# Moving evictions and rotations, and changing two matmul shapes, in the latent attention of a two-block layer on one core

## The chip, the cores and the metric

One Trainium2 chip, of which the program uses one core. The time is that of one execution on the device in microseconds; the figure of a kernel is the median of its runs. The profile is one further execution. TensorE (PE; PEld in the views is its weight loads) multiplies, VectorE (DVE) and ScalarE (ACT) work on elements, GpSimd (POOL) and SyncE (SP) issue transfers.

## What is computed

A sequence of 256 tokens with 2048 channels goes through one block (modulation, gated spatial unit, long convolution, feed-forward) and then a second one of two layers: a pooling mixer and a latent attention. The change touches only the latter, here cut to what matters:

```python
def mla_mixer(xn, cos, sin, w_in, q_norm, w_uq, kv_norm, w_ukv, w_out):
    z = xn @ w_in                       # q_lat 512, kv_lat 512, k_pe 64, g 2048
    q = (rms_norm(q_lat, q_norm) @ w_uq).reshape(B, S, 16, 192)
    kv = (rms_norm(kv_lat, kv_norm) @ w_ukv).reshape(B, S, 16, 256)
    q_nope, q_pe = q[..., :128], q[..., 128:]
    k_nope, v = kv[..., :128], kv[..., 128:]
    q_pe = rope(q_pe, cos, sin)         # 64 channels, for each head
    k_pe = rope(k_pe, cos, sin)         # 64 channels, one for all heads
    q = concatenate([q_nope, q_pe]); k = concatenate([k_nope, k_pe for each head])
    o = causal_block_attention(q, k, v)
    return (o * silu(g)) @ w_out
```

A head's score is thus a product over 128 channels and one over 64, added.

## The kernel before

Every engine runs a program written out by hand; semaphores tie them together. All weights are float32 and are streamed in units of 128 partitions x 2048 (1 MB) through four buffers raw. ScalarE rounds each half of a unit to w_hi (`round_half`, line 1371) and VectorE takes the difference w_lo (`rest_half`, line 1950). The activations are split in the same way, and each product is three matmuls: lo x hi, hi x hi, hi x lo (`products`, lines 786 to 788). There are four buffers of w_hi and w_lo each, a half-unit in each, so that ScalarE can cast a half once TensorE has used the one four halves ahead of it.

`run` walks over a stage's chunks on ScalarE and VectorE: first the rounding of the chunk c, then the function `hook(i, c)`. In the stages w_uq (6 chunks of 512 columns) and w_ukv (8 chunks) a chunk is one unit, 24 matmuls of 128x512, and it ends in one of two pairs of PSUM banks. `latent_out` copies a finished pair to q_tm or kv_tm (tokens on partitions) and so frees it for the chunk after the next; before, VectorE does that in the hook of the next chunk (`copy_pair`, line 2348).

The stages around the change, in order: mla_in (the two latents, 512 columns each), k_pe (the 64 columns of the rotary key, lines 1218 to 1243), w_uq (queries), w_ukv (keys and values), mla_g (the gate, 16 units), w_out. In k_pe the activations are the stationary operand, so that the key comes out with tokens on partitions, and VectorE scales it by the tokens' inverse norm (line 2700).

From w_ukv's chunk 3 on TensorE puts a step of the heads behind each unit (`head_step`): it turns head s (`head_turn`, lines 1250 to 1253: q, k and the 64 rotary channels), forms the scores of head s-1 (`head_score`: line 1266 over 128 channels, line 1267 over the 64 rotary ones, for 128 and 256 keys), turns the probabilities of head s-2 (line 1275) and multiplies with the values of head s-3 (lines 1286 to 1288). `head_drain` is the other engines' part: ScalarE copies the turned q and k (line 1871), the turned probabilities (1887) and forms the exponentials (1879); VectorE copies the turned rotary part to q_peT (line 2735), scales and masks the scores and takes their maximum (2742 to 2747), and divides the output (2754). `head_turn` of a head waits for the copies of the head before it, q_peT among them.

The rotation (`rotate_heads(t)`) works on one tile of 128 tokens and all 16 heads, six instructions of VectorE. Both tiles and the rotary key are rotated in the first hooks of w_ukv.

## Time and profile before

| | us |
|---|---|
| median of 3 runs | 2838.79 (2838.48 to 2839.21) |
| the profiled execution's own time | 2840.93 |
| its span, first to last instruction | 2839.6 |
| TensorE busy | 2704.3 (95%), 12651 matmuls |
| VectorE busy | 1807.9 (64%) |
| ScalarE busy | 1257.4 (44%) |
| mean granted clock of TensorE | 0.977 |

The busy time of TensorE has modelled ends, so 95% does not say that it works at its peak. The granted clock is given as a share of the full one: 1.00 is 2.4 GHz, 0.50 is 1.2 GHz. The attention's part that the change touches lies between 2377 and 2620 us. In the rows of a timeline stand start, length, engine, line and operation, output <- inputs, shape, the count of merged instructions, and in brackets the idle time before and what ended it ("issue": nothing that the profile shows).

### The profile page before, as it was taken

Reading aid. Unit: us, or ns where it says so; the run is one execution under the profiler, and the core shown is the slowest. Engines: PE = TensorE matmul, PEld = TensorE weight load, DVE = VectorE, ACT = ScalarE, POOL = GpSimd, SP = SyncE. Lnnn points to the kernel's source line nnn. Section 1 sums busy time; section 2 is a strip of 40 time slices with the busy share of each in tenths; the row PEclk is TensorE's granted clock in tenths of the full one; section 3 lists DMA queues with packets and bytes.
Section 4 is the critical chain, followed back from the end, with each engine's and each line's share of the span. In section 5 each row is a group of like instructions: output and inputs, shape, how many; then the busy total and the mean of one; then the engine's idle time right before and its main releaser. Section 6 shows DMA issues by size and latency. Waiting matters only on the chain.

```text
span 2839.6 us, 31582 instructions
## 1 busy us (share of the span) xinstructions
PE 2704.3 (95%) x12651; PEld 2226.8 (78%) x12651; DVE 1807.9 (64%) x1795; ACT 1257.4 (44%) x1524; POOL 67.5 (2%) x67
## 2 busy tenths in 40 slices
PE   2679999999999999999999899999999999899999
PEld 1368997777878888888888788888888888677887
DVE  6666856776887654468766844555654664645665
ACT  0044443333434444465555433444444654335464
POOL 2300000000000000000000000000000000000000
PEclk9789999999999999999999999999999998999999
DMA  8688667768877875566555555555565554523554
GB/s 315 237 300 302 238 210 247 268 243 291 324 252 278 279 238 187 183 200 204 193 193 193 195 175 169 179 186 178 201 197 194 186 182 137 162 91 113 199 179 148
DMA packets 258084, 599.46 MB, mean 211 GB/s; under 512 B 12243, under 2 KB 14942, under 8 KB 243422
## 3 DMA queue, kind: packets, MB, share of 16 engines
q1 hardware_dynamic: 246848, 561.55, 58.2%
q0 software_dynamic: 4848, 23.64, 2.4%
q10 hardware_dynamic: 6254, 12.40, 1.3%
q8 instruction: 94, 1.54, 0.2%
q14 instruction: 40, 0.33, 0.0%
HBM read 587.07 MB, written 10.49 MB: 210 GB/s over the span
## 4 chain that ended last, share of the span: by engine, by line
PE 88%; DVE 7%; issue 1%; ACT 1%; DMA 1%; POOL 1%; ACTq 0%; DVEq 0%; POOLq 0%
PE ps L786 25%; PE ps L787 25%; PE ps L788 25%; DVE ada_acc L1978 2%; PE ps L886 1%; PE ps L870 1%; PE ps L873 1%; PE ps L872 1%; DVE w_lo L1950 1%; PE ps L1031 1%; PE ps L1022 1%; PE ps L947 1%; PE ps L1267 1%; PE ps L1266 1%; PE ps L903 1%
## 5 line engine op out<-in xcount | busy, mean ns | idle before, releaser
L1950 DVE TENSOR_TENSOR w_lo<-raw,w_hi 128x1024 fp32r<-128x1024 f32 x870 | 1051.3, 1221 | 743.0 <-ACT w_hi L1371 741.5
L1371 ACT CAST w_hi<-raw 128x1024 fp32r<-128x1024 f32 x870 | 908.6, 1051 | 1174.8 <-PE ps L788 1046.6
L786 PE MATMUL ps<-w_lo,x_hi 128*128 128x512 f32 x2592 | 1020.4, 394 | 8.8 <-DVE w_lo L1950 4.9
L788 PE MATMUL ps<-w_hi,x_lo 128*128 128x512 f32 x2592 | 1011.3, 390 | 0.0
L787 PE MATMUL ps<-w_hi,x_hi 128*128 128x512 f32 x2592 | 1011.1, 390 | 0.0
L786 PEld LDWEIGHTS ps<-w_lo,x_hi 128*128 128x128 f32 x2592 | 488.1, 188 | 112.8 <-issue 8.1
L788 PEld LDWEIGHTS ps<-w_hi,x_lo 128*128 128x128 f32 x2592 | 487.9, 188 | 102.6
L787 PEld LDWEIGHTS ps<-w_hi,x_hi 128*128 128x128 f32 x2592 | 488.3, 188 | 100.3 <-issue 1.2
L1978 DVE SCALAR_TENSOR_TENSOR ada_acc<-raw,cond,ada_acc 128x2048 f32<-128x2048 f32 x96 | 236.1, 2459 | 6.6 <-DMA raw<-in_w_ada 3.7
L786 PE MATMUL ps<-w_lo,pooled_hi 128*128 128x512 f32 x384 | 151.0, 393 | 2.5 <-DVE w_lo L1950 2.5
L788 PE MATMUL ps<-w_hi,pooled_lo 128*128 128x512 f32 x384 | 149.5, 389 | 0.0
L787 PE MATMUL ps<-w_hi,pooled_hi 128*128 128x512 f32 x384 | 149.5, 389 | 0.0
L870 PE MATMUL ps<-x_hi,w_lo 128*128 128x256 f32 x384 | 110.1, 287 | 5.4 <-DVE w_lo L1950 5.4
L872 PE MATMUL ps<-x_hi,w_hi 128*128 128x256 f32 x384 | 109.7, 286 | 0.0
L873 PE MATMUL ps<-x_lo,w_hi 128*128 128x256 f32 x384 | 109.7, 286 | 0.0
L786 PEld LDWEIGHTS ps<-w_lo,pooled_hi 128*128 128x128 f32 x384 | 72.1, 188 | 19.8 <-DVE w_lo L1950 5.2
L788 PEld LDWEIGHTS ps<-w_hi,pooled_lo 128*128 128x128 f32 x384 | 72.1, 188 | 15.2
L787 PEld LDWEIGHTS ps<-w_hi,pooled_hi 128*128 128x128 f32 x384 | 72.1, 188 | 14.4
L2401 DVE TENSOR_TENSOR x_lo<-ff,x_hi 128x1024 fp32r<-128x1024 f32 x64 | 77.9, 1217 | 7.4 <-ACT x_hi L1665 7.4
L870 PEld LDWEIGHTS ps<-x_hi,w_lo 128*128 128x128 f32 x384 | 74.8, 195 | 5.8 <-DVE w_lo L1950 5.8
L872 PEld LDWEIGHTS ps<-x_hi,w_hi 128*128 128x128 f32 x384 | 74.8, 195 | 0.0
L873 PEld LDWEIGHTS ps<-x_lo,w_hi 128*128 128x128 f32 x384 | 74.7, 195 | 0.0
(335 smaller groups left out, 2125.5 us busy)
## 6 DMA issues: line engine op xcount, KB each, us to landing
raw<-in_w_m SPq DMA_DIRECT2D x128, 1024.0 KB, 5.1
raw<-in_w_ada SPq DMA_DIRECT2D x96, 1024.0 KB, 5.0
raw<-in_w_in SPq DMA_DIRECT2D x72, 1024.0 KB, 5.7
raw<-in_pool_w_in SPq DMA_DIRECT2D x64, 1024.0 KB, 5.3
raw<-in_pool_w_out SPq DMA_DIRECT2D x32, 1024.0 KB, 5.0
raw<-in_ple_w_gate SPq DMA_DIRECT2D x32, 1024.0 KB, 5.1
raw<-in_mla_w_in SPq DMA_DIRECT2D x24, 1024.0 KB, 5.2
raw<-in_w_o SPq DMA_DIRECT2D x16, 1024.0 KB, 6.8
```

The costliest lines, as they stand in the source:

```text
L786: mm(bank, xh, wl, start=start, stop=False)
L787: mm(bank, xh, wh, start=False, stop=False)
L788: ins = mm(bank, xl, wh, start=False, stop=stop)
L870: mm(to, wl, x_hi[:, k, :], start=k == 0 and ct % 2 == 0, stop=False, skip_group_check=True)
L872: mm(to, wh, x_hi[:, k, :], start=False, stop=False, skip_group_check=True)
L873: ins = mm(to, wh, x_lo[:, k, :], start=False, stop=k == KT - 1, skip_group_check=True)
L886: ins = nc.tensor.transpose(fm_ps[slot][:, k, t * P:(t + 1) * P], src[:, t, (4 * q + k) * P:(4 * q + k + 1) * P], ident[:])
L903: ins = mm(ps[:, bank, k:k + 1], acc[ADA_ACC[b]][:, k * P:(k + 1) * P], ones[:, 0:1], start=True, stop=True)
L1371: nc.scalar.copy(by_ktile(st, w_hi[st.half_slot(j, half)][:, 0:n]), raw_half(st, j, half)).then_inc(hi_split, 1)
L1950: tt(by_ktile(st, w_lo[slot][:, 0:n]), raw_half(st, j, half), by_ktile(st, w_hi[slot][:, 0:n].bitcast(F32)), ALU.subtract).then_inc(lo_spl ...
L1978: stt(out=buf[:], in0=raw[st.slot(j)][:], scalar=cond[:, ds(kk, 1)], in1=buf[:], op0=ALU.mult, op1=ALU.add).then_inc(ada_added, 1)
L2401: tt(x_lo[:, s:s + 4], ff[:, 4 * u:4 * u + 4], x_hi[:, s:s + 4].bitcast(F32), ALU.subtract).then_inc(fm_lo, 1)
```

## The change

- The stage k_pe makes the weights the stationary operand (128 rows, 64 columns) and streams both token tiles at once (256 columns); the key comes out with channels on partitions. VectorE copies it to k_peT, TensorE turns it behind w_uq's chunk 1, VectorE scales it in hook 2 and rotates it in hook 3, and TensorE turns it back behind w_uq's chunk 4 (before: behind w_ukv's chunk 2).
- The lower 64 rows of q_peT (both buffers) and k_peT are set to zero once, and the scores' second product takes all 128 rows.
- `latent_out` goes from VectorE to ScalarE (`nc.scalar.copy`), for all 14 chunks. On ScalarE it stands behind the head's part of the same hook.
- On VectorE the rotation of the queries is cut into four pieces (8 heads, one token tile each), in the hooks 4 and 5 of w_uq and 1 and 2 of w_ukv.

TensorE, the rotary key. Before, from the turned latent on; each pair of three belongs to one token tile:

```order
L886 MATMUL ps<-ident,lat 128x128 x8
L1229 MATMUL ps<-w_lo_57,x_hi 128x64
L1230 MATMUL ps<-w_hi_53,x_hi 128x64
L1231 MATMUL ps<-w_hi_53,x_lo 128x64
L1229 MATMUL ps<-w_lo_57,x_hi 128x64
```

and now (the shape is that of the output):

```order
L887 MATMUL ps<-ident,lat 128x128 x8
L1228 MATMUL ps<-x_hi,w_lo_57 64x256
L1229 MATMUL ps<-x_hi,w_hi_53 64x256
L1230 MATMUL ps<-x_lo,w_hi_53 64x256
L1228 MATMUL ps<-x_hi,w_lo_57 64x256
```

There were 96 such rows, and there are 48; x and w have changed places.

VectorE, from the end of w_uq into w_ukv's first chunks. Before:

```order
L2348 COPY q_tm<-ps 128x2x512
L2682 TENSOR_TENSOR rope_t<-q_tm,rope_cos 128x512
L2682 TENSOR_TENSOR rope_t<-q_tm,rope_sin 128x512
L2682 TENSOR_TENSOR rope_t<-q_tm,rope_cos 128x512
L2682 TENSOR_TENSOR rope_t<-q_tm,rope_sin 128x512
L2684 TENSOR_TENSOR q_tm<-rope_t 128x16x32
L2685 TENSOR_TENSOR q_tm<-rope_t 128x16x32
L1950 TENSOR_TENSOR w_lo_57<-raw_51,w_hi_53 128x1024
L1950 TENSOR_TENSOR w_lo_58<-raw_51,w_hi_54 128x1024
L2348 COPY kv_tm<-ps 128x2x512
```

and now:

```order
L1975 TENSOR_TENSOR w_lo_57<-raw_51,w_hi_53 128x1024
L1975 TENSOR_TENSOR w_lo_58<-raw_51,w_hi_54 128x1024
L2703 TENSOR_TENSOR rope_t<-q_tm,rope_cos 128x256
L2703 TENSOR_TENSOR rope_t<-q_tm,rope_sin 128x256
L2703 TENSOR_TENSOR rope_t<-q_tm,rope_cos 128x256
L2703 TENSOR_TENSOR rope_t<-q_tm,rope_sin 128x256
L2705 TENSOR_TENSOR q_tm<-rope_t 128x8x32
L2706 TENSOR_TENSOR q_tm<-rope_t 128x8x32
L1975 TENSOR_TENSOR w_lo_59<-raw_52,w_hi_55 128x1024
```

The copies are gone from this queue, and a rotation has half the width.

ScalarE, w_ukv's hooks 5 and 6, the first heads. Before:

```order
L1871 COPY qk_fm_150<-ps 128x512
L1371 CAST w_hi_55<-raw_52 128x1024
L1371 CAST w_hi_56<-raw_52 128x1024
L1871 COPY qk_fm_151<-ps 128x512
L1879 ACT_TABLE_LOAD
L1879 ACTIVATE prob_158,sm_sum<-score_154,sm_max 128x128
L1879 ACTIVATE prob_158,sm_sum<-score_154,sm_max 128x256
L1371 CAST w_hi_53<-raw_49 128x1024
```

and now:

```order
L1887 COPY qk_fm_150<-ps 128x512
L1871 COPY kv_tm<-ps 128x2x512
L1376 CAST w_hi_55<-raw_52 128x1024
L1376 CAST w_hi_56<-raw_52 128x1024
L1887 COPY qk_fm_151<-ps 128x512
L1895 ACT_TABLE_LOAD
L1895 ACTIVATE prob_158,sm_sum<-score_154,sm_max 128x128
L1895 ACTIVATE prob_158,sm_sum<-score_154,sm_max 128x256
L1871 COPY kv_tm<-ps 128x2x512
L1376 CAST w_hi_53<-raw_49 128x1024
```

The copies of kv_tm stand between a head's part and the next casts.

```diff
--- before.py
+++ after.py
@@ -254,7 +254,7 @@
     q_tm = at("q_tm", 120, [2, HEADS, QK])
     kv_tm = at("kv_tm", 144, [2, HEADS, NOPE + VD])
     lat = at("lat", 144, [2, 2, CH])
-    rope_t = at("rope_t", 112, [4, HEADS, ROPE // 2])
+    rope_t = at("rope_t", 112, [4, HEADS // 2, ROPE // 2])
     mla_sig = [at(f"mla_sig{c}", 190 if c < 3 else 112, [2, CH]) for c in range(4)]
     o0_hi = at("o0_hi", 190, [4, S], F32R)
     o0_lo = at("o0_lo", 194, [4, S], F32R)
@@ -423,6 +423,7 @@
     prob_turned = sem("prob_turned")
     probT_out = sem("probT_out")
     k_peT_out = sem("k_peT_out")
+    k_pe_turned = sem("k_pe_turned")
     o_mm = sem("o_mm")
     o_ready = sem("o_ready")
     out_stored = sem("out_stored")
@@ -1223,12 +1224,10 @@
             for q in range(8):
                 wh, wl = (w[slot][:, q * ROPE:(q + 1) * ROPE] for w in (w_hi, w_lo))
                 k = 8 * half + q
-                for t in range(2):
-                    xh, xl = (x[:, k, t * P:(t + 1) * P] for x in (x_hi, x_lo))
-                    bank = ps[:, t, 0:ROPE]
-                    mm(bank, xh, wl, start=k == 0, stop=False)
-                    mm(bank, xh, wh, start=False, stop=False)
-                    ins = mm(bank, xl, wh, start=False, stop=k == KT - 1)
+                bank = ps[0:ROPE, 0, 0:S]
+                mm(bank, wl, x_hi[:, k, :], start=k == 0, stop=False)
+                mm(bank, wh, x_hi[:, k, :], start=False, stop=False)
+                ins = mm(bank, wh, x_lo[:, k, :], start=False, stop=k == KT - 1)
             ins.then_inc(half_used, 1)
         pe.wait_ge(fm_empty, 62)
         for n in range(6):
@@ -1238,6 +1237,16 @@
             if n == 0:
                 pe.wait_ge(lat_ready, 2)
                 turn(62, lat[:, :, 1], 0)
+            if n == 1:
+                for t in range(2):
+                    ins = nc.tensor.transpose(ps[:, 7, S + t * ROPE:S + (t + 1) * ROPE],
+                                              k_peT[0:ROPE, t * P:(t + 1) * P], ident[0:ROPE, 0:ROPE])
+                ins.then_inc(k_pe_turned, 1)
+            if n == 4:
+                pe.wait_ge(rope_done, 1)
+                for t in range(2):
+                    ins = nc.tensor.transpose(ps[0:ROPE, 7, t * P:(t + 1) * P], k_pe[:, t, :], ident[:])
+                ins.then_inc(k_peT_ready, 1)
 
         def head_turn(h):
             pe.wait_ge(pair_empty, 95 + h // 2 + 1)
@@ -1264,7 +1273,7 @@
                 keys = slice(0, (t + 1) * P)
                 bank = ps[:, 5, t * P:(2 * t + 1) * P]
                 mm(bank, qk[:, 0, t * P:(t + 1) * P], qk[:, 1, keys], start=True, stop=False)
-                ins = mm(bank, qp[0:ROPE, t * P:(t + 1) * P], k_peT[0:ROPE, keys], start=False, stop=True)
+                ins = mm(bank, qp[:, t * P:(t + 1) * P], k_peT[:, keys], start=False, stop=True)
             ins.then_inc(scored, 1)
 
         def head_prob(h):
@@ -1302,13 +1311,9 @@
             pe.wait_ge(pair_empty, 95 + n - 1)
             for half in range(2):
                 products(ST["w_ukv"], 0, n, half, 2 * half, kv_hi, kv_lo, pair((95 + n) % 2), half == 0, half == 1)
-            if n == 2:
-                pe.wait_ge(rope_done, 1)
-                for t in range(2):
-                    ins = nc.tensor.transpose(ps[0:ROPE, 7, t * P:(t + 1) * P], k_pe[:, t, :], ident[:])
-                ins.then_inc(k_peT_ready, 1)
             if n == 3:
                 pe.wait_ge(k_peT_out, 1)
+                pe.wait_ge(rope_done, 5)
             if n >= 3:
                 head_step(n - 3)
         st = ST["mla_g"]
@@ -1858,7 +1863,18 @@
             latent_root(1)
         run(ST["k_pe"], 0, k_pe_hook)
 
+        q_flat = q_tm[:].rearrange("p t h d -> p t (h d)")
+        kv_flat = kv_tm[:].rearrange("p t h d -> p t (h d)")
+
+        def latent_out(st, n, m, to):
+            act.wait_ge(half_used, chunk_end(st, 0, n))
+            nc.scalar.copy(to[:, :, cols(n)], ps[:, 2 * (m % 2):2 * (m % 2) + 2, :]).then_inc(pair_empty, 1)
+
         def w_uq_hook(i, c):
+            if c:
+                if c == 1:
+                    act.wait_ge(pair_empty, 89)
+                latent_out(ST["w_uq"], c - 1, 89 + c - 1, q_flat)
             if c == 2:
                 direct(62, kv_hi[:], fm_b[:, COL["kv_norm"]:COL["kv_norm"] + 4])
         run(ST["w_uq"], 0, w_uq_hook)
@@ -1895,7 +1911,14 @@
             if 0 <= step - 1 < HEADS:
                 head_exp(step - 1)
 
-        run(ST["w_ukv"], 0, lambda i, c: head_drain(c - 5) if c >= 5 else None)
+        def w_ukv_hook(i, c):
+            if c >= 5:
+                head_drain(c - 5)
+            if c == 0:
+                latent_out(ST["w_uq"], 5, 94, q_flat)
+            else:
+                latent_out(ST["w_ukv"], c - 1, 95 + c - 1, kv_flat)
+        run(ST["w_ukv"], 0, w_ukv_hook)
 
         def mla_sigmoid(c):
             st, m = ST["mla_g"], 103 + c
@@ -1910,6 +1933,8 @@
         def mla_g_hook(n):
             def hook():
                 head_drain(n + 3)
+                if n == 1:
+                    latent_out(ST["w_ukv"], 7, 102, kv_flat)
                 if n in (6, 10, 14):
                     mla_sigmoid((n - 6) // 4)
             return hook
@@ -2665,16 +2690,12 @@
         run(ST["mla_in"], 0, mla_in_hook, tail=mla_in_tail)
 
         def k_pe_hook(i, c):
+            for part in (q_peT[0], q_peT[1], k_peT):
+                nc.vector.memset(part[ROPE:P, :], 0.0)
             latent_in(1)
             direct_rest(61, DIRECT["q"], q_hi[:], q_lo[:], fm_b[:, COL["q_norm"]:COL["q_norm"] + 4])
             latent_norm(1)
         run(ST["k_pe"], 0, k_pe_hook)
-
-        q_flat = q_tm[:].rearrange("p t h d -> p t (h d)")
-        kv_flat = kv_tm[:].rearrange("p t h d -> p t (h d)")
-
-        def latent_out(st, n, m, to):
-            copy_pair(st, 0, n, m % 2, to[:, :, n * CH:(n + 1) * CH])
 
         def rotate(x1, x2, cos, sin, scratch, done=None):
 
@@ -2688,39 +2709,43 @@
             else:
                 ins.then_inc(done, 1)
 
-        def rotate_heads(t):
-            x = q_tm[:, t, :, NOPE:QK]
-            cos, sin = (tb[:, t].unsqueeze(1).to_broadcast([P, HEADS, ROPE // 2]) for tb in (rope_cos, rope_sin))
-            rotate(x[:, :, 0:ROPE // 2], x[:, :, ROPE // 2:ROPE], cos, sin, lambda n: rope_t[:, n])
+        def rotate_heads(part):
+
+            half, t = part // 2, part % 2
+            dve.wait_ge(rope_done, 1 + part)
+            if t == 0:
+                dve.wait_ge(pair_empty, 92 + 3 * half)
+            x = q_tm[:, t, 8 * half:8 * half + 8, NOPE:QK]
+            cos, sin = (tb[:, t].unsqueeze(1).to_broadcast([P, HEADS // 2, ROPE // 2]) for tb in (rope_cos, rope_sin))
+            rotate(x[:, :, 0:ROPE // 2], x[:, :, ROPE // 2:ROPE], cos, sin, lambda n: rope_t[:, n], rope_done)
 
         def w_uq_hook(i, c):
             if c == 0:
                 dve.wait_ge(half_used, end(ST["k_pe"]))
-                for t in range(2):
-                    ins = tsc(k_pe[:, t], ps[:, t, 0:ROPE], rms[:, RMS_H2, 2, t:t + 1], None, ALU.mult)
-                ins.then_inc(pair_empty, 1)
-            else:
-                latent_out(ST["w_uq"], c - 1, 89 + c - 1, q_flat)
+                nc.vector.tensor_copy(k_peT[0:ROPE, :], ps[0:ROPE, 0, 0:S]).then_inc(pair_empty, 1)
             if c == 2:
                 direct_rest(62, DIRECT["kv"], kv_hi[:], kv_lo[:], fm_b[:, COL["kv_norm"]:COL["kv_norm"] + 4])
-        run(ST["w_uq"], 0, w_uq_hook)
-
-        def w_ukv_hook(i, c):
-            if c == 0:
-                latent_out(ST["w_uq"], 5, 94, q_flat)
-                dve.wait_ge(pair_empty, 95)
+                dve.wait_ge(k_pe_turned, 1)
+                for t in range(2):
+                    ins = tsc(k_pe[:, t], ps[:, 7, S + t * ROPE:S + (t + 1) * ROPE], rms[:, RMS_H2, 2, t:t + 1], None,
+                              ALU.mult)
+                then(ins)
+            if c == 3:
                 dve.wait_ge(sines, 2)
-                rotate_heads(0)
-            else:
-                latent_out(ST["w_ukv"], c - 1, 95 + c - 1, kv_flat)
-            if c == 1:
-                rotate_heads(1)
-            if c == 2:
                 rotate(k_pe[:, :, 0:ROPE // 2], k_pe[:, :, ROPE // 2:ROPE], rope_cos[:], rope_sin[:],
                        lambda n: rope_t[:, n, 0:2], rope_done)
             if c == 4:
+                rotate_heads(0)
+            if c == 5:
                 dve.wait_ge(k_peT_ready, 1)
                 nc.vector.tensor_copy(k_peT[0:ROPE, :], ps[0:ROPE, 7, 0:S]).then_inc(k_peT_out, 1)
+                rotate_heads(1)
+        run(ST["w_uq"], 0, w_uq_hook)
+
+        def w_ukv_hook(i, c):
+            if c in (1, 2):
+                rotate_heads(1 + c)
+            if c == 4:
                 dve.wait_ge(mask_ready, 2)
             if c >= 5:
                 head_drain(c - 5)
@@ -2780,8 +2805,6 @@
 
         def mla_g_hook(n):
             def hook():
-                if n == 1:
-                    latent_out(ST["w_ukv"], 7, 102, kv_flat)
                 head_drain(n + 3)
                 if n in (6, 10, 14):
                     mla_gated((n - 6) // 4)
```

## Rows read from the trace of the kernel before

**Rows 1.** The page: engines of the chain that ended last.
```profile
PE 88%; DVE 7%; issue 1%; ACT 1%; DMA 1%; POOL 1%; ACTq 0%; DVEq 0%; POOLq 0%
```

**Rows 2.** Windows: start:end, length, busy (instructions) per engine, PEclk (1.00 is full), DMA.
```profile
2377.30:2382.00 4.70, 4.70 (x46) 4.70 (x43) 3.60 (x10) 4.18 (x11) 0.00 (x0) 1.00 0.01 4
2382.40:2399.00 16.60, 16.60 (x67) 15.47 (x67) 4.64 (x6) 2.48 (x3) 0.00 (x0) 0.50 0.26 74
2399.60:2477.40 77.80, 68.76 (x313) 55.18 (x311) 51.80 (x63) 28.06 (x34) 0.00 (x0) 1.00 0.49 157
2478.20:2484.20 6.00, 6.00 (x16) 4.02 (x16) 2.23 (x2) 1.75 (x3) 0.00 (x0) 0.50 0.43 125
2484.80:2491.20 6.40, 3.56 (x16) 2.62 (x14) 2.73 (x6) 0.23 (x1) 0.00 (x0) 1.00 0.03 12
2491.80:2501.20 9.40, 9.40 (x30) 6.98 (x29) 3.83 (x10) 4.09 (x10) 0.00 (x0) 0.50 0.00 0
2502.00:2620.00 118.00, 118.00 (x604) 93.16 (x603) 65.28 (x137) 56.47 (x110) 0.00 (x0) 1.00 0.36 116
```

**Rows 3.** Timeline, weight loads: start, length; first of the rotary key, first of w_uq.
```profile
2377.48 0.19 PEld L1229 LDWEIGHTS ps<-w_lo,x_hi 128*128 128x128 f32 x1
...
2393.70 0.33 PEld L786 LDWEIGHTS ps<-w_lo,q_hi 128*128 128x128 f32 x1
```

**Rows 4.** Windows: split 128x256 (lines 870 to 873), float32 128x256 (line 1031), split 128x512.
```profile
300.00:310.00 10.00, 10.00 (x85) 10.00 (x84) 7.70 (x6) 3.14 (x3) 0.00 (x0) 1.00 0.95 343
471.53:474.99 3.46, 3.46 (x18) 3.03 (x16) 2.02 (x3) 1.04 (x1) 0.00 (x0) 1.00 0.79 290
2415.00:2429.00 14.00, 14.00 (x63) 11.58 (x63) 9.38 (x9) 5.26 (x5) 0.00 (x0) 1.00 0.71 222
```

**Rows 5.** Waits of weight loads from 2370 to 2620: total us, times, longest.
```profile
PEld ps L1250 <- issue: 6.9, 2, 3.4
...
PEld ps L786 <- issue: 3.7, 3, 1.9
...
PEld ps L1250 <- DVE kv_tm L2348: 2.1, 1, 2.1
PEld ps L1250 <- DVE k_peT L2723: 2.1, 1, 2.1
```

**Rows 6.** Timeline, VectorE: rotation ahead of weights; evictions ahead of a head.
```profile
2431.48 0.69 DVE L2682 TENSOR_TENSOR rope_t<-q_tm,rope_cos 128x512 f32<-128x512 f32 x1
...
2435.34 2.36 DVE L1950 TENSOR_TENSOR w_lo<-raw,w_hi 128x1024 fp32r<-128x1024 f32 x2
...
2473.55 1.22 DVE L2348 COPY kv_tm<-ps 128x1024 f32<-128x1024 f32 x1 [6.33 <-PE ps L788]
...
2475.99 0.41 DVE L2735 COPY q_peT<-ps 64x256 f32<-64x256 f32 x1
```

**Rows 7.** Timeline, weight loads of one head at full clock.
```profile
2533.18 0.22 PEld L1253 LDWEIGHTS ps<-ident,q_tm 128*64 128x64 f32 x2
2533.40 0.30 PEld L1266 LDWEIGHTS ps<-qk_fm 128*128 128x128 f32 x2
2533.82 0.29 PEld L1267 LDWEIGHTS ps<-k_peT,q_peT 64*128 64x128 f32 x2
...
2534.87 0.29 PEld L1267 LDWEIGHTS ps<-k_peT,q_peT 64*128 64x128 f32 x2 [0.33 <-issue]
2535.49 0.31 PEld L1275 LDWEIGHTS ps<-ident,prob 128*128 128x128 f32 x3 [0.33 <-issue]
```

**Rows 8.** Groups of instructions, ScalarE: busy us, mean ns | idle before.
```profile
L1371 ACT CAST w_hi<-raw 128x1024 fp32r<-128x1024 f32 x868 | 907.4, 1052 | 1172.6 <-PE ps L788 1044.4 <-PE ps L873 75.3 <-DMA raw<-in_w_in 15.3
...
L1767 ACT COPY proj<-ps 128x1024 f32<-128x1024 f32 x8 | 8.1, 1010 | 2.6 <-PE ps L788 2.6
```

**Rows 9.** Timeline, VectorE: latent before the rotary key; low part of kv.
```profile
2376.91 1.41 DVE L2648 TENSOR_SCALAR lat<-ps,rms 128x512 f32<-128x512 f32 x2 [4.10 <-PE ps L788]
...
2409.60 1.65 DVE L2009 SCALAR_TENSOR_TENSOR kv_lo<-ps,fm_b,kv_hi 128x256 fp32r<-128x256 f32 x4
```

## Prediction

> **What bounds the kernel now.** I read the chain that ended last first: TensorE holds 88% of it and VectorE 7% [rows 1]. A stage counts, then, where TensorE stands still or runs slowly. The windows over the stretch that the change touches (2377 to 2620) show both [rows 2]. Over 2382.4 to 2399.0 the granted clock is 0.50, which is the 1.2 GHz level, although TensorE is busy without a gap there and in the 4.7 us ahead of it. It is 0.50 again over 2478.2 to 2484.2 and 2491.8 to 2501.2. Between these, at 1.00, TensorE is idle for 77.80 - 68.76 = 9.0 us and 6.40 - 3.56 = 2.8 us. From 2502 on it is busy throughout at 1.00. The weight loads tell more than the matmuls, whose ends are modelled: the time from one load's start to the next is what an instruction really costs, and the waits of the loads show the stalls [rows 5, 7]. Everything else of the kernel keeps its order.
>
> **1. The rotary key's stage.** Now 16 k-tiles x 2 token tiles x 3 products = 96 matmuls with 64 moving columns; afterwards 16 x 3 = 48 with 256 moving columns and 64 stationary ones. Today the stage lasts from the first load of line 1229 to the first load of w_uq, 2393.70 - 2377.48 = 16.2 us [rows 3]. The nearest row for the new form is the split product with 128x256: 84 loads in 10.00 us at clock 1.00, 0.119 us each [rows 4]. 48 x 0.119 = 5.7 us. **-10.5 us.** If the clock is at 0.50 for the whole stage it is 11.4 us and the gain 4.8; if it goes at the pace of the 43 loads that stand in the 4.70 us before the fall [rows 2], 0.109 us each, it is 5.2 us and the gain 11.0.
> What was hidden under the 16.2 us has to stay hidden under 5.7: q_lo, the second latent and the first weights of w_uq. VectorE starts this work at 2376.91 [rows 9] and the window to 2382.0 holds most of it; after it come two low parts of weights in 2.36 us [rows 6]. I put the first at 2383.2, where TensorE now arrives (2377.5 + 5.7). So no wait, or a few tenths. The three memsets of 64x256 have no row; VectorE is idle 4.1 us in front of 2376.91 [rows 9], where they stand, and three copies of that shape are 3 x 0.41 = 1.2 us [rows 6], so they cost nothing unless they took over 1.4 us each. The copy of the unscaled key (0.41) stands behind low parts that TensorE needs later; it costs nothing.
>
> **2. The clock behind that stage.** From 2393.70 to 2399.0 the first products of w_uq run at 0.50 [rows 2, 3]. If the clock does not fall, half of 5.3 is returned: **-2.6 us** (bounds 0 and -2.6). The clock fell 4.6 us or so into a stage of matmuls with 64 moving columns; stretches of 256 moving columns ran at 1.00 [rows 4]. I take the small matmuls to be the cause.
>
> **3. Stalls in w_ukv.** The waits of the loads are 6.9 + 2.1 + 2.1 and, of the 3.7, what is left without one 0.33 that belongs to a head: 3.4; together 14.5 us in six stalls [rows 5]. By the matmuls' busy time it is 9.0 + 2.8 = 11.9 [rows 2]. I take 13.2. They have two causes on VectorE. (a) Rotation of all 16 heads stands in front of low parts of weights: from 2431.48 to 2435.34, 3.9 us, twice [rows 6]. (b) In front of a head VectorE waits for a chunk's end, evicts it for 1.22 us, then does a head's scores, and the copy of q_peT that TensorE waits for ends at 2476.4, 2.9 us after the chunk's end at 2473.5 [rows 6]. Afterwards ScalarE evicts, and the head's work is ahead of that. Can ScalarE carry it? From a chunk's end: copy 1.01, cast 1.05 [rows 8], low part 1.2 [rows 6], with a few tenths of signalling 3.6 us; the second half 4.7. A chunk is 24 matmuls at 14.00 / 63 = 0.222 us, 5.3 us [rows 4]. So the next chunk's first half is ready 1.7 us early, and the second later still in need. ScalarE's copies of a head and its exponentials stand where TensorE also spends its own head step. At w_uq's chunk 3 the margin goes: the high part of kv on ScalarE is taken as long as the low part on VectorE, 1.65 us [rows 9], and then VectorE does that low part and scales the key (about 0.5), 1.0 + 1.65 + 1.65 + 0.5 + 1.2 = 6.0 us against 5.3 and two transposes of 0.6: I charge 0.3 (part 6). The rotation in pieces is four times about half of 3.9, 2 us each, in front of weights whose cast is not done until 2.1 us after the chunk's end; VectorE reaches these pieces before the chunk's end. What is late next in w_ukv is thus nothing on VectorE, but the chunk itself. **-13.2 us** (bounds -6, if the order removes only half, and -14.5).
>
> **4. The clock in w_ukv.** Both low stretches begin within 2 us behind the two longest stalls (3.4 us each [rows 5]). 6.0 + 9.4 = 15.4 us at 0.50 [rows 2]; half comes back with the stalls gone: **-7.7 us** (bounds 0 and -8.5 with the edges).
>
> **5. Scores over 128 rows.** Within a head the loads start at 2533.40, 2533.82, ..., 2534.87, and the next operation at 2535.49: 2.09 us for four products [rows 7]. Two float32 loads with 128 columns and no change of rows take 2533.40 - 2533.18 = 0.22; one with 256 takes 3.46 / 16 = 0.216, two 0.43 [rows 4, 7]. Four products would be 0.22 + 0.22 + 0.43 + 0.43 = 1.30. The rest, 0.79 us or 0.20 for each of four passages between 128 and 64 rows, stands in the rows as a load that isn't pulled ahead (0.33 idle). With zeros in the lower 64 rows all four have 128 rows: 16 x 0.79 = **-12.7 us**, all on TensorE's path, which has no idle time beyond 2502 [rows 2]. Bounds: 0, if the rows are not the cause, and -12.7. VectorE and ScalarE must keep up with heads 0.8 us shorter: in 118 us they are busy 65 and 56 [rows 2], so they do.
> By the Trainium skill (TensorE: Matmul & The Clock Gate, Why this matters for your kernels) a matmul over few rows takes the same time as one over 128. By that rule this term would be 0. The rows speak only partly against it: the pause lies at the passage, not in the 64-row matmul.
>
> **6. Added.** Two transposes over 64 rows of the unscaled key: 0.22 and two passages, 0.6 us. Wait at chunk 3: 0.3. The transposes of the rotated key only move from w_ukv to w_uq. **+0.9 us** (0 to +3, if ScalarE's signalling is slower than I think at the fourteen evictions).
> The weights come earlier as well: 1 MB in 5.3 us is some 200 GB/s, where other stretches get 343 [rows 4]. No cost.
>
> **Sum.** -10.5 - 2.6 - 13.2 - 7.7 - 12.7 + 0.9 = -45.8 us. The profiled execution's span of 2839.6 becomes 2793.8, its time of 2840.9 becomes 2795.1. The median of the runs, 2838.8, is 2.1 below that execution and becomes **2793.0**.
>
> **The rivals.** (A) The passage of rows is not what holds the loads. For it: the rows show only that the pause comes with the 64-row products, which are also the only ones that read k_peT and q_peT; against it: the pause also stands in front of the products behind them, which read other tiles. Then term 5 is 0: 2793.0 + 12.7 = 2805.7. This is the case that the rule above gives.
> (B) The clock falls again, in the new key stage or at the first heads. For it: half of the array's columns hold nothing in the new stage, and no row shows such a stretch of 5.7 us. Against it: rows 4. The fall would come after some 4.6 us and last until about as far into w_uq as now (5.3 us): 6 to 7 us at half rate, 3.3 lost; at the heads one stretch like those of now costs 3.0 to 4.7 [rows 2]. 2796 to 2801, middle 2798. The Trainium skill (TensorE: Matmul & The Clock Gate, The HAM clock gate) has the clock fall after idle time only. The fall at 2382 had none ahead of it, so this trace does not agree; by the page the shape would not matter and the fall could come as before.
> (C) The new order leaves a stall in w_ukv: ScalarE's exponential waits for VectorE's maximum, and the eviction stands behind it. Half of terms 3 and 4 are lost: 6.6 + 3.9 = 10.5, so 2803.5.
> (D) Slower. ScalarE's eviction becomes what TensorE waits for at each of the fourteen chunks: copy, cast and low part in a row, each behind the chunk's end. The cover is 5.3 us and the chain 3.6. Beyond 5.3 each microsecond costs 14; terms 3 and 4 would be lost first, and from a chain of 5.3 + 45.8 / 14 = 8.6 us on the kernel is slower than before. At 9.5 us it would be 14 x 0.9 = 13 us slower, 2852. Nothing in rows 8 is near that.
>
> **How the numbers follow.** Forecast 0.68, A 0.11, B 0.11, C 0.07, D 0.03. The forecast's own uncertainty, from terms 1, 3 and 6, is 2790 to 2797. The range goes to A and C, which leaves out D and mishaps that coincide: 2789 to 2807. About 0.2% (5.7 us) is what a measurement of this kernel can tell from no change. All cases but D are beyond it: faster 0.96, same 0.01, slower 0.03.
>
> **What would show it.** In the new profile: the key's stage in 5 to 6 us between first load and first load of w_uq, clock 1.00 there and to 2500; no wait of loads for q_peT or for low parts over 1 us in w_ukv; a head's four products in 1.3 us; ScalarE's copies of q_tm and kv_tm at 1.0 us each. The forecast is wrong if the clock shows 0.50 in any of these windows, if the loads behind 128-row scores still show 0.33 idle, or if ScalarE's casts follow a chunk's end by more than 4 us.

## The result

The changed kernel takes 2794.2 us (median of 4 runs, 2792.6 to 2795.8), the kernel before 2838.6 (4 runs, 2835.7 to 2839.2); the ratio is 0.9845, 95% interval 0.9828 to 0.9862. The forecast was 2793.0 with a range of 2789 to 2807. The profiled execution took 2792.6 with a span of 2791.3.

The page of the changed kernel, busy time and the chain that ended last:

```profile
PE 2671.2 (96%) x12605; PEld 2210.3 (79%) x12605; DVE 1794.2 (64%) x1797; ACT 1268.7 (45%) x1538; POOL 67.5 (2%) x67
...
PE 89%; DVE 7%; ACT 1%; issue 1%; DMA 1%; POOL 1%; ACTq 0%; DVEq 0%; POOLq 0%
```

TensorE's busy time is 33.1 us less, VectorE's 13.7 less and ScalarE's 11.3 more than in the table of before: the copies have changed engines. In the chain TensorE's share is now 89%, where it was 88% [rows 1].

The same kind of windows as in [rows 2], over the key's stage, the start of w_uq, the rest up to the first head, and the heads:

```profile
2374.30:2379.90 5.60, 5.60 (x50) 5.39 (x48) 4.50 (x11) 5.35 (x12) 0.00 (x0) 1.00 0.00 0
2380.10:2396.00 15.90, 15.90 (x74) 12.91 (x75) 7.19 (x10) 8.05 (x12) 0.00 (x0) 1.00 0.60 199
2396.00:2436.30 40.30, 40.25 (x179) 33.00 (x178) 29.28 (x50) 20.93 (x22) 0.00 (x0) 1.00 0.58 183
2436.40:2582.40 146.00, 146.00 (x799) 125.17 (x798) 85.46 (x172) 83.89 (x151) 0.00 (x0) 1.00 0.40 130
```

PEclk is 1.00 in all four, where it was 0.50 for 32.0 us in [rows 2], and TensorE is idle for 0.05 us in 207.8. Timeline of the weight loads (first of the key, first of w_uq, and the two loads with a wait):

```profile
2374.21 0.14 PEld L1228 LDWEIGHTS ps<-x_hi,w_lo 128*64 128x64 f32 x1
...
2380.03 0.19 PEld L787 LDWEIGHTS ps<-w_lo,q_hi 128*128 128x128 f32 x1 [0.33 <-issue]
...
2392.08 0.20 PEld L1242 LDWEIGHTS ps<-ident,k_peT 64*128 64x128 f32 x2 [0.35 <-issue]
...
2398.12 0.19 PEld L787 LDWEIGHTS ps<-w_lo,q_hi 128*128 128x128 f32 x1 [0.44 <-issue]
```

The key's stage lasts 2380.03 - 2374.21 = 5.82 us (16.22 in [rows 3]). And one head, to be read beside [rows 7]:

```profile
2483.64 0.22 PEld L1262 LDWEIGHTS ps<-ident,q_tm 128*64 128x64 f32 x2
2483.85 0.30 PEld L1275 LDWEIGHTS ps<-qk_fm 128*128 128x128 f32 x2
2484.07 0.30 PEld L1276 LDWEIGHTS ps<-k_peT,q_peT 128*128 128x128 f32 x2
2484.30 0.30 PEld L1275 LDWEIGHTS ps<-qk_fm 128*128 128x128 f32 x2
2484.63 0.41 PEld L1276 LDWEIGHTS ps<-k_peT,q_peT 128*128 128x128 f32 x2
2485.06 0.47 PEld L1284 LDWEIGHTS ps<-ident,prob 128*128 128x128 f32 x3
2485.49 0.30 PEld L1295 LDWEIGHTS ps<-kv_tm,probT 128*128 128x128 f32 x2
```

The four products are 0.22, 0.23, 0.33 and 0.43 apart and the next operation's load comes 1.21 us after the first, not 2.09. All waits of weight loads from 2370 to 2620, where there were 14.5 us and more [rows 5]:

```profile
PEld ps L787 <- issue: 0.8, 2, 0.4
PEld ps L787 <- DVE w_lo L1975: 0.4, 1, 0.4
PEld ps L1242 <- issue: 0.4, 1, 0.4
```

For all that follows I cut the trace into four stretches, from first load to first load: the key's stage, w_uq, w_ukv up to the first head's transposes, and the heads up to the last load of their value products. They tell more than the times: the key's stage begins anywhere from 2374.2 to 2379.0 us in the profiled executions, in kernels that are the same up to there, while a stretch in which the clock stays at 1.00 repeats within some hundredths from kernel to kernel. Where the clock falls, a stretch is that of one execution, and how far it would vary isn't known. In us:

| kernel | key | w_uq | to first head | heads | sum | median (runs) |
|---|---|---|---|---|---|---|
| before | 16.22 | 36.10 | 27.21 | 173.73 | 253.26 | 2838.6 (4) |
| changed | 5.82 | 34.56 | 21.76 | 146.06 | 208.20 | 2794.2 (4) |
| e1 | 16.36 | 36.53 | 21.76 | 146.01 | 220.66 | 2807.0 (4) |
| e2 | 5.81 | 34.55 | 21.76 | 146.06 | 208.18 | 2795.9 (1) |
| e3 | 5.81 | 34.58 | 21.76 | 157.68 | 219.83 | 2806.9 (4) |
| e4 | 5.82 | 34.19 | 21.76 | 157.05 | 218.82 | 2803.8 (4) |
| e5 | 5.81 | 34.20 | 21.75 | 146.06 | 207.82 | 2797.0 (1) |
| e6 | 5.82 | 34.57 | 22.19 | 146.06 | 208.64 | 2793.8 (1) |
| e7 | 5.81 | 34.57 | 21.76 | 151.83 | 213.97 | 2800.8 (1) |
| e8 | 16.33 | 35.93 | 27.22 | 155.91 | 235.39 | 2822.4 (4) |
| e9 | 11.25 | 34.56 | 21.77 | 146.05 | 213.63 | 2799.7 (1) |
| e10 | 10.72 | 34.05 | 21.76 | 146.02 | 212.55 | 2797.6 (1) |
| e11 | 5.81 | 34.23 | 21.76 | 172.36 | 234.16 | 2822.0 (4) |
| e12 | 16.22 | 36.08 | 27.24 | 157.50 | 237.04 | 2823.4 (1) |

The change's stretches are shorter by 253.26 - 208.20 = 45.1 us. The spans differ by 48.3, of which 3.3 lie ahead of the change (2377.48 against 2374.21); the rest of the kernel behind the heads takes the same time.

### The profile page after: what moved, and what is told of

Same layout as the page of the kernel before. It is cut to its first block, busy times and chain, and to the rows that moved or that the text cites. A ratio compares the mean times of both kernels' runs of the same rounds, so it can differ in the third digit from the quotient of the medians.

```text
span 2791.3 us, 31507 instructions
## 1 busy us (share of the span) xinstructions
PE 2671.2 (96%) x12605; PEld 2210.3 (79%) x12605; DVE 1794.2 (64%) x1797; ACT 1268.7 (45%) x1538; POOL 67.5 (2%) x67
## 4 chain that ended last, share of the span: by engine, by line
PE 89%; DVE 7%; ACT 1%; issue 1%; DMA 1%; POOL 1%; ACTq 0%; DVEq 0%; POOLq 0%
PE ps L787 26%; PE ps L789 25%; PE ps L788 25%; DVE ada_acc L2003 2%; PE ps L887 2%; PE ps L871 1%; PE ps L874 1%; PE ps L873 1%; DVE w_lo L1975 1%; PE ps L1032 1%; PE ps L1023 1%; PE ps L948 1%; PE ps L904 1%; DMA raw<-in_w_in 0%; DMA rows_d<-in_ln_b 0%
## 5 line engine op out<-in xcount | busy, mean ns | idle before, releaser
L788 PEld LDWEIGHTS ps<-w_hi,pooled_hi 128*128 128x128 f32 x384 | 72.1, 188 | 14.5
```

The costliest lines, as they stand in the source:

```text
L788: mm(bank, xh, wh, start=False, stop=False)
```

## The experiments

**e1: the key's stage as before, in the changed kernel.**

```diff
-                bank = ps[0:ROPE, 0, 0:S]
-                mm(bank, wl, x_hi[:, k, :], start=k == 0, stop=False)
-                mm(bank, wh, x_hi[:, k, :], start=False, stop=False)
-                ins = mm(bank, wh, x_lo[:, k, :], start=False, stop=k == KT - 1)
+                for t in range(2):
+                    xh, xl = (x[:, k, t * P:(t + 1) * P] for x in (x_hi, x_lo))
+                    bank = ps[:, t, 0:ROPE]
+                    mm(bank, xh, wl, start=k == 0, stop=False)
+                    mm(bank, xh, wh, start=False, stop=False)
+                    ins = mm(bank, xl, wh, start=False, stop=k == KT - 1)
```

The key then has tokens on partitions at once; VectorE scales it in w_uq's hook 0 and the two transposes behind chunk 1 go.

> The changed kernel with the rotary key's stage as before (96 matmuls, activations stationary, 64 moving columns). Theory (the small matmuls bring the clock down): the stage takes about 16.2 us, the clock falls to 0.50 some 4.6 us into it and stays there for about 5 us of w_uq; +10.4 +2.6 us against the changed kernel's 2794.2, so 2807. Rival (the fall had another cause, gone with the rest of the change): clock 1.00, 96 loads of 0.11 us are 10.6 us, +4.8 us, so 2799.

Measured 2807.0 (2805.9 to 2808.4), ratio to the kernel before 0.9885 (0.9869 to 0.9902). Windows: the stage's beginning, its rest, the beginning of w_uq:

```profile
2376.00:2380.50 4.50, 4.50 (x42) 4.50 (x42) 3.40 (x10) 4.33 (x11) 0.00 (x0) 0.98 0.00 0
2382.00:2392.00 10.00, 10.00 (x48) 10.00 (x49) 0.66 (x1) 1.04 (x1) 0.00 (x0) 0.50 0.33 107
2392.00:2396.40 4.40, 4.40 (x13) 3.53 (x13) 2.74 (x4) 1.04 (x1) 0.00 (x0) 0.50 0.01 2
```

The stage is 16.36 us and the clock falls in it, with no stall anywhere near and with the rest of the change in place. Stage, clock and time come out as the theory had them. Whether the 64 moving columns are the cause is tested further in e2, e9 and e10.

**e2: weights stationary, but the two token tiles apart.** The number of matmuls is that of before, with 128 moving columns and loads of 64 columns.

```diff
-                bank = ps[0:ROPE, 0, 0:S]
-                mm(bank, wl, x_hi[:, k, :], start=k == 0, stop=False)
-                mm(bank, wh, x_hi[:, k, :], start=False, stop=False)
-                ins = mm(bank, wh, x_lo[:, k, :], start=False, stop=k == KT - 1)
+                for t in range(2):
+                    xh, xl = (x[:, k, t * P:(t + 1) * P] for x in (x_hi, x_lo))
+                    bank = ps[0:ROPE, t, 0:P]
+                    mm(bank, wl, xh, start=k == 0, stop=False)
+                    mm(bank, wh, xh, start=False, stop=False)
+                    ins = mm(bank, wh, xl, start=False, stop=k == KT - 1)
```

> The changed kernel, but the key's stage streams the two token tiles apart: 96 matmuls with 128 moving columns, weights still stationary with 64 columns. Both theories give 96 x 0.11 = 10.6 us at full clock. Theory (what brings the clock down is the narrow moving operand of 64 columns): clock 1.00, stage 10.6 us, +4.8 us. Rival (many short matmuls bring it down, whatever their columns, or the half-empty array): the clock falls to 0.50 some 4.6 us into the stage, which takes 14 to 16 us, +10 us or more with w_uq's slow start.

A window that covers nearly all of the stage:

```profile
2377.70:2383.30 5.60, 5.60 (x96) 5.60 (x95) 4.50 (x11) 5.36 (x12) 0.00 (x0) 1.00 0.02 3
```

Both expected lengths missed: the stage takes 5.81 us, 0.061 us for a matmul, as long as with 48 of twice the columns. The 0.11 us of a matmul in the old form at full clock was the load of 128 stationary columns (e10 has the same 128 moving columns with that load, at 0.11 us); with 64 stationary columns it is gone. What term 1 gains beyond the clock is thus in the smaller stationary operand, not in the number of matmuls. The clock stays at 1.00, so neither the number of matmuls nor the half-empty array is enough to bring it down.

**e9: weights stationary, 64 moving columns.** Four quarters of the tokens, 192 matmuls; to find room in PSUM two quarters are added into one place, so the rotary key is not computed.

```diff
-                bank = ps[0:ROPE, 0, 0:S]
-                mm(bank, wl, x_hi[:, k, :], start=k == 0, stop=False)
+                for t in range(4):
+                    xh, xl = (x[:, k, t * ROPE:(t + 1) * ROPE] for x in (x_hi, x_lo))
+                    bank = ps[0:ROPE, t % 2, 0:ROPE]
+                    mm(bank, wl, xh, start=k == 0 and t < 2, stop=False)
...
```

> The changed kernel, key's stage with weights stationary (64 columns) and 192 matmuls of 64 moving columns; two quarters of the tokens are added into one place, so the rotary key is not computed, the work else is the same. e2 showed that a matmul with a 64-column load and 128 moving columns takes 0.061 us, so a 64-column load is not above that. Theory (64 moving columns bring the clock down): it falls some 4.6 us into the stage; 192 x 0.055 to 0.06 = 10.6 to 11.5 us at full clock become 15 to 18. Rival (it is the time in which nothing is streamed, about three quarters before and half or less here): clock 1.00, stage 10.6 to 11.5 us.

```profile
2376.00:2387.00 11.00, 11.00 (x191) 11.00 (x190) 5.64 (x11) 6.01 (x12) 0.00 (x0) 1.00 0.27 91
```

11.25 us for 192, 0.059 each, clock 1.00 throughout: 64 moving columns do not bring the clock down by themselves. The theory as I had put it falls; in this run the rival's forecast came true.

**e10: activations stationary as before, 128 moving columns.** The second 64 are the next k-tile's weights and are not used.

```diff
-                wh, wl = (w[slot][:, q * ROPE:(q + 1) * ROPE] for w in (w_hi, w_lo))
+                wh, wl = (w[slot][:, q * ROPE:(q + 2) * ROPE] for w in (w_hi, w_lo))
...
-                    bank = ps[:, t, 0:ROPE]
+                    bank = ps[:, t, 0:2 * ROPE]
```

(with the rest of e1's edit)

> The changed kernel with the key's stage of before (activations stationary, 128 columns loaded, 96 matmuls) but 128 moving columns, of which the second 64 are not used. A load of 128 columns bounds each at 0.11 us, so the array streams nothing for about half of it. Theory (64 moving columns bring the clock down): clock 1.00, stage 96 x 0.11 = 10.6 us, +4.8 us against the changed kernel. Rival (time in which nothing is streamed, while loads take over): clock 0.50 after some 4.6 us, 16 us, as with 64 columns.

```profile
2374.80:2385.40 10.60, 10.60 (x97) 10.60 (x96) 5.67 (x11) 6.02 (x12) 0.00 (x0) 1.00 0.25 80
```

10.72 us, clock 1.00; here it is the theory's forecast that came true. So a load of 128 columns for each matmul does not bring it down either; only the two together, a load of 128 columns for 64 that stream (e1, and before), do. The forms of e1 and e10 differ by 64 moving columns and nothing else; what in them the chip goes by, these runs don't show. A curious result follows: twice the columns streamed, with the same loads, took 10.72 us where half of them took 16.36. The two runs also divide the gain of the new stage: 16.36 - 10.72 = 5.6 us of it are the clock and 10.72 - 5.81 = 4.9 us the smaller loads.

**e3: scores over 64 rows, in the changed kernel.**

```diff
-                ins = mm(bank, qp[:, t * P:(t + 1) * P], k_peT[:, keys], start=False, stop=True)
+                ins = mm(bank, qp[0:ROPE, t * P:(t + 1) * P], k_peT[0:ROPE, keys], start=False, stop=True)
```

> The changed kernel with the scores' second product over 64 rows again. Theory (a passage between 128 and 64 rows keeps the next weight load from being pulled ahead): 0.33 idle before loads returns, a head's step is 0.72 us longer, 16 heads give +11.6 us, so 2806. Rival (the rows do not matter): 0, 2794.

2806.9 (2806.0 to 2808.1), ratio 0.9883 (0.9867 to 0.9900). The heads' stretch is 157.68 - 146.06 = 11.62 us longer. Waits of the weight loads:

```profile
PEld ps L1276 <- issue: 5.3, 16, 0.3
PEld ps L1284 <- issue: 5.0, 15, 0.3
```

One wait of 0.33 in front of each head's last 64-row product and one in front of the operation behind it, as in [rows 7]. The rows are the cause; rival A of the prediction is excluded.

**e4: evictions on VectorE, ahead of the head's work.** In VectorE's hooks (and none on ScalarE):

```diff
+            else:
+                latent_out(ST["w_uq"], c - 1, 89 + c - 1, q_flat)
...
         def w_ukv_hook(i, c):
+            if c == 0:
+                latent_out(ST["w_uq"], 5, 94, q_flat)
+            else:
+                latent_out(ST["w_ukv"], c - 1, 95 + c - 1, kv_flat)
             if c in (1, 2):
                 rotate_heads(1 + c)
```

> The changed kernel with all 14 evictions on VectorE again, ahead of the head's work as before; rotation stays in pieces and early. Theory (evictions ahead of a head's work made the stalls at the heads, and these the low clock): stalls of 2.1, 3.4 and 3.4 us before the transposes of heads 1 to 3 and about 15 us at clock 0.50, in all some +16 us, so 2810. Rival (the rotation alone had put VectorE behind): at most +2 us, clock 1.00.

2803.8 (2802.7 to 2807.4), ratio 0.9872 (0.9856 to 0.9888). Timeline, the loads that wait, and two windows:

```profile
2448.46 0.14 PEld L1259 LDWEIGHTS ps<-ident,q_tm 128*128 128x128 f32 x1 [2.12 <-DVE kv_tm L2359]
...
2459.13 0.18 PEld L1259 LDWEIGHTS ps<-ident,q_tm 128*128 128x128 f32 x1 [3.43 <-issue]
...
2472.95 0.14 PEld L1259 LDWEIGHTS ps<-ident,q_tm 128*128 128x128 f32 x1 [3.44 <-issue]
```

```profile
2458.20:2465.00 6.80, 5.84 (x21) 5.04 (x22) 3.14 (x5) 3.83 (x8) 0.00 (x0) 0.50 0.11 10
...
2473.00:2490.00 17.00, 17.00 (x95) 14.67 (x96) 10.70 (x21) 8.43 (x19) 0.00 (x0) 1.00 0.19 63
```

The three stalls are back to the hundredth. The clock falls once, for 6.8 us, from 0.9 us before the end of the first stall of 3.43 us on, and not at the second. In before it was low for 17 us at the heads, and half of the difference, 5 us, is why the stalls cost 11.0 us here and not 16. The other stretches show no stall at all: with the rotation in pieces and early, VectorE bears the evictions there.

**e5: evictions on VectorE, behind the head's work.** As e4, but in w_ukv's hooks and the gate's hook 1 `latent_out` stands after `head_drain`.

> The changed kernel with all 14 evictions on VectorE, but behind the head's work in each hook of w_ukv. It tells the order from the engine. If the order alone makes the gain at the heads: no stall over 1 us there, clock 1.00, 0 to +1 us against the changed kernel. If the engine matters too (VectorE waits for the chunk's end with the next head's work queued behind it): stalls of 1 to 3 us stay.

```profile
PEld ps L787 <- DVE w_lo L1961: 0.4, 1, 0.4
PEld ps L1242 <- issue: 0.4, 1, 0.4
...
PEld ps L787 <- issue: 0.3, 1, 0.3
```

No stall at the heads, clock 1.00, heads 146.06 us. The order alone makes this gain; ScalarE isn't needed for it. The sum of the stretches is even 0.4 us below the changed kernel's, since the wait at w_uq's chunk 3 is gone. In the time that can't be told: its one run of 2797.0 had the key's stage begin at 2378.96, 4.8 us later than the changed kernel's profiled execution.

**e7: ScalarE evicts, ahead of the head's work.**

```diff
-            if c >= 5:
-                head_drain(c - 5)
             if c == 0:
                 latent_out(ST["w_uq"], 5, 94, q_flat)
             else:
                 latent_out(ST["w_ukv"], c - 1, 95 + c - 1, kv_flat)
+            if c >= 5:
+                head_drain(c - 5)
```

and the same exchange in the gate's hook 1.

> The changed kernel with ScalarE's eviction ahead of the head's part of each hook. Theory (an eviction waits for a chunk's end, and everything of the head behind it comes late): qk_fm and the exponentials come after the chunk's end, so the head's transposes and probabilities are waited for, about 1 us and more at each of the first three heads, and the clock may fall; +3 to +12 us. Rival (ScalarE has slack enough in either order): 0 to +1 us.

```profile
PEld ps L1259 <- ACT kv_tm L1871: 6.1, 3, 2.0
```

Three stalls of 2.0 us and +5.8 us, with the clock at 1.00: the same mistake on the other engine. e5 and e7 together cross the two: what counts is what stands behind a wait for a chunk's end, on whichever engine.

**e6: the rotation in two lumps, in w_ukv's hooks 0 and 1.**

The two pieces in w_uq's hooks 4 and 5 go, and:

```diff
-            if c in (1, 2):
-                rotate_heads(1 + c)
+            if c in (0, 1):
+                rotate_heads(2 * c)
+                rotate_heads(2 * c + 1)
```

> The changed kernel with the queries' rotation in two lumps of two pieces each, in w_ukv's hooks 0 and 1, as before; ScalarE evicts. Theory (the rotation ahead of low parts made the two early stalls, 1.5 and 1.9 us): one or two waits for low parts of about 1 us each, since the eviction of 1.2 us no longer stands in that queue too; +1 to +3 us. Rival (the eviction made them): 0.

+0.4 us, all in the stretch to the first head (22.19 against 21.76). The rotation of 3.9 us alone fits under a chunk; and evictions on VectorE beside a rotation in pieces stall nothing there either (e4: 21.76). So it was late before only together with the evictions of 1.2 us in the same queue. Cutting it up brings 0.4 us.

**e8: the kernel before with scores over 128 rows.** e3's line turned round, and three memsets behind the key's rotation.

> The kernel before with the scores over 128 rows alone (three memsets on VectorE more, behind the key's rotation, where it is already late). Theory: the stalls and the low clock stay, the heads are shorter by 0.72 us each: -11.6 us and up to 1 us back for the memsets, so 2828. Rival (the passages of rows, not the stalls, bring the clock down at the heads): the clock stays at 1.00 there and it gains 7 us more, 2820.

2822.4 (2820.4 to 2824.8), ratio 0.9940 (0.9924 to 0.9957), 16 to 17 us less than before where 11.6 was expected. Windows around the third and fourth head:

```profile
2478.00:2485.00 7.00, 4.33 (x20) 3.24 (x18) 2.84 (x7) 0.06 (x1) 0.00 (x0) 1.00 0.47 150
2486.60:2489.90 3.30, 3.30 (x14) 2.82 (x14) 1.34 (x4) 0.75 (x3) 0.00 (x0) 0.50 0.00 0
2490.00:2500.00 10.00, 10.00 (x56) 8.56 (x55) 6.89 (x15) 4.69 (x12) 0.00 (x0) 1.00 0.34 105
```

The stalls are there (3.43 and 3.44 us), but the low clock at the heads has shrunk from 17 us to 3.4. The time lies between theory and rival: in this execution the shorter heads come with most of the low clock gone. That the rows are the reason for that is not shown by it alone; see what stays open.

**e11: evictions on VectorE ahead of the head's work, scores over 64 rows.** The edits of e4 and e3 together.

> The changed kernel with both undone: evictions on VectorE ahead of the head's work (e4) and scores over 64 rows (e3). If the two only add up: heads' stretch 157.05 + 157.68 - 146.06 = 168.7 us. If the pauses of the 64-row scores behind a stall also keep the clock low for longer (before: 173.7 us with some 16 us at 0.50): about 173, and the low stretches are longer than e4's 7.5 us. Time 2815 in the first case, 2820 in the second.

2822.0 (2819.9 to 2822.9), ratio 0.9937 (0.9921 to 0.9954). Waits of the loads, and two windows:

```profile
PEld ps L1259 <- issue: 6.9, 2, 3.4
...
PEld ps L1259 <- DVE kv_tm L2359: 2.1, 1, 2.1
```

```profile
2461.80:2468.50 6.70, 6.70 (x18) 4.55 (x17) 2.10 (x2) 1.61 (x3) 0.00 (x0) 0.50 0.49 155
...
2475.40:2482.10 6.70, 6.70 (x23) 4.80 (x21) 1.71 (x6) 2.27 (x8) 0.00 (x0) 0.50 0.01 2
```

The heads take 172.36 us, not 168.7: there are two low stretches of 6.8 us, where e4 had one and before one of 6.8 and one of 10.2. The length is that of the second case; its reason, that the pauses of the 64-row scores keep the clock low, is not shown by it.

**e12: the kernel before, its evictions at the heads behind the head's work.**

```diff
-            else:
+            elif c < 5:
                 latent_out(ST["w_ukv"], c - 1, 95 + c - 1, kv_flat)
...
             if c >= 5:
                 head_drain(c - 5)
+                latent_out(ST["w_ukv"], c - 1, 95 + c - 1, kv_flat)
```

and the same exchange in the gate's hook 1.

> The kernel before with one thing changed: in w_ukv's hooks from 5 on and in the gate's hook 1 VectorE evicts behind the head's work instead of ahead of it. Theory (the order alone makes the stalls at the heads, as e5 says from the other side): the three stalls of 2.1, 3.4 and 3.4 us go and with them the low clock at the heads; the heads' stretch falls from 173.7 to e3's 157.7 us, -16 us, so about 2823. Rival (the early rotation's delay on VectorE still shows): one or two stalls of 1 to 2 us stay.

```profile
PEld ps L1267 <- issue: 5.3, 16, 0.3
PEld ps L1275 <- issue: 5.0, 15, 0.3
...
PEld ps L786 <- issue: 3.7, 3, 1.9
...
PEld ps L1250 <- DVE k_peT L2723: 2.1, 1, 2.1
```

The heads' stretch falls by 16.2 us to 157.50, 2823.4 in its one run, by moving one call over another. The three stalls ahead of the heads (1.5, 1.9 and 2.1 us) stay, and so does the pause of the 64-row scores. The third of them, 2.1 us of waiting for k_peT, is the same mistake once more: in hook 4 the copy of the key that the first head needs stands behind the eviction. The theory's numbers come out.

## Why the prediction was right, term by term

The sum was -45.8 us, and the stretches give -45.1.

- **Term 1** (-10.5): 16.22 to 5.82, -10.4. Right in size. The row that I took the price from was the wrong kind: [rows 4]'s 0.119 us belongs to loads of 128 columns, and the new form has 64; there 256 streamed columns set the time, 0.113 us from load to load. 48 of these are 5.4 us, and a wait of 0.33 us ahead of w_uq's first load, which the sum didn't have, makes 5.8. That the two prices lie so close together was luck.
- **Term 2** (-2.6) and the new work in w_uq (+0.9): 36.10 to 34.56, so -1.5 net; of it the transposes that come from w_ukv are another 0.3 us. Both parts right in size: e1 against e10, w_uq with a slow start and without one, is 36.53 - 34.05 = 2.5 us. The cause was put too simply, and this is the step of the prediction that failed in its mechanism: not the 64 moving columns but these together with loads of 128 (e1, e9, e10). The number held because the new stage has neither.
- **Term 3** (-13.2): to the first head 27.21 to 21.76, of which 0.3 are the transposes that moved: -5.1. At the heads three stalls of 2.12, 3.43 and 3.44; e7, where 6.1 us of waits cost 5.8, says that about 8.5 of these 9.0 count. Together -13.6. Right, and so was the reading of the two causes, except that the rotation alone would not have stalled anything (e6), and that the third stall, on k_peT, is of the second kind.
- **Term 4** (-7.7): before against e12, whose heads have the same matmuls, is 16.2 us, less 8.5 for the stalls: -7.7. Right, as far as a difference to an estimate can say. But it does not stand by itself: it is there in full only with 64-row scores.
- **Term 5** (-12.7): 11.6 by e3. This is the term that was mis-sized, by 0.07 us a head (16 x 0.79 is 12.6; the sum carried 12.7). I charged all four passages at 0.20. Between the loads of [rows 7] 2.09 us became 1.21, even more than the 0.79, but the transposes of the probabilities behind them take longer: 0.43 us from their first load to the value product's, where it was 2535.77 - 2535.49 = 0.28 in the trace of before. 0.88 less 0.15 is the 0.73 that e3 measured. My reading, which no run tests, is that the last passage's pause partly covered time that the 256-column product in front needs anyway.
- **Term 6** (two transposes 0.6, wait at chunk 3 0.3): w_uq of e10, which has the wait but not the transposes, is 34.56 - 34.05 = 0.5 us shorter. The wait is 0.44 in the rows above, 0.36 by e5 against the changed kernel. ScalarE does the eviction, the high part of kv and then the casts,

```profile
2392.19 1.02 ACT L1871 COPY q_tm<-ps 128x1024 f32<-128x1024 f32 x1 [3.39 <-PE ps L789]
2393.10 1.57 ACT L1440 ACTIVATE kv_hi<-ps,fm_b 128x256 fp32r<-128x256 f32 x4
2394.53 2.03 ACT L1376 CAST w_hi<-raw 128x1024 fp32r<-128x1024 f32 x2
```

and VectorE, which waits for the high part, the low part, the key's scaling and then the weights:

```profile
2394.70 1.66 DVE L2034 SCALAR_TENSOR_TENSOR kv_lo<-ps,fm_b,kv_hi 128x256 fp32r<-128x256 f32 x4 [4.46 <-ACT kv_hi L1440]
2396.28 0.47 DVE L2730 TENSOR_SCALAR k_pe<-ps,rms 128x64 f32<-128x64 f32 x2
2396.78 2.36 DVE L1975 TENSOR_TENSOR w_lo<-raw,w_hi 128x1024 fp32r<-128x1024 f32 x2
```

These are the five pieces of the working, in that order and near those lengths: 5.8 us from the copy's start to the end of the first low part of weights, where 6.0 was worked out.

That the terms add up hides that two of them overlap. The heads' stretch in all four combinations:

| | stalls | no stalls |
|---|---|---|
| 64 rows | 173.73 (before), 172.36 (e11) | 157.50 (e12), 157.68 (e3) |
| 128 rows | 155.91 (e8), 157.05 (e4) | 146.06 (changed) |

With the stalls in place the rows bring 17.8 us (before to e8) or 15.3 (e11 to e4), without them 11.4 to 11.6; the order brings 16.2 or 14.7 with 64 rows and 9.9 to 11.0 with 128. Together they bring 27.7. The clock is the reason. In before it was low at the heads for 6.8 and 10.2 us:

```profile
2477.80:2484.50 6.70, 6.70 (x17) 4.46 (x17) 2.36 (x2) 2.15 (x4) 0.00 (x0) 0.50 0.43 131
...
2491.40:2501.60 10.20, 10.19 (x31) 7.70 (x32) 4.23 (x10) 4.49 (x11) 0.00 (x0) 0.50 0.00 0
```

In e11 it was twice 6.8, in e4 6.8 and in e8 3.4. Half of the difference between before and e8 is 6.8 us, where the rows brought 6.2 to 6.4 more than without stalls; half of that between e11 and e4 is 3.4, where they brought 3.7 to 3.9 more. Taken in the order in which I put them (stalls, clock, then rows) the terms are right; taken the other way round, by e8, term 5 would be 17.8 and term 4 only 1.4.

**The rivals.** A (rows not the cause) is excluded by e3. By the Trainium skill's rule (TensorE: Matmul & The Clock Gate, Why this matters for your kernels) a matmul over few rows takes as long as one over 128. These rows don't contradict it for the product itself, whose two loads over 64 rows follow at 0.11 us as those over 128 do at 128 streamed columns; the waits stand at the changes between the two, ahead of the 64-row load and ahead of the 128-row one behind it, which that rule doesn't cover. They cost 0.72 us a head (e3). B (clock falls again) didn't happen in any run of the new stage; e9 and e10 keep it as well. C (a stall through the order on ScalarE) is what e7 produces when the order is turned; in the change's order ScalarE's waits for the maximum cost TensorE nothing. D was nowhere near. At a chunk of w_ukv, where the copy starts at the chunk's end, the chain is

```profile
2431.34 1.01 ACT L1871 COPY kv_tm<-ps 128x1024 f32<-128x1024 f32 x1 [2.53 <-PE ps L789]
...
2433.33 2.36 DVE L1975 TENSOR_TENSOR w_lo<-raw,w_hi 128x1024 fp32r<-128x1024 f32 x2 [3.08 <-ACT w_hi L1376]
```

so both halves are ready 2435.69 - 2431.34 = 4.35 us after it, where 4.7 was worked out; the first is ready after about 3.2, where 3.6 was.

**What stays open.** Why the clock falls at one stall of 3.4 us and not at another (e4, e8) is not settled, nor why the low stretch is shorter with 128 rows; that the pauses of the 64-row scores prolong it would fit all four cells, but was only argued. A rival is untested: the moment. The low stretches begin anywhere from 0.9 us before to 1.7 us after a stall's end, and shorter heads move the stalls too (the first long stall of e8 ends 98.2 us after the key's stage began, that of before 99.0). Each length is that of one profiled execution. The runs' mean granted clock differs within one kernel, in before from 0.977 to 0.979, and 0.002 of 2839 us is some 11 us at half clock, somewhere in the kernel; so the low stretches need not repeat. The times of e4 and e8 spread over 4.7 and 4.4 us against 3.2 for the changed kernel. For the key's stage the fall stands in four traces (before, e1, e8, e12); that it stays away in the forms of e2, e9 and e10 rests on one execution each. No version beats the changed one by more than can be measured; e5's order on VectorE gives 0.4 us in the stretches.
